# A decoder's first stage: operands loaded channels first, a halved first unit, and squares taken later

## The reference

```python
# first block, twice
h = rms_norm(x, norm_g[l])
proj = h @ w_in[l]                 # q_a, k_a, v_a, z_a, c_q, c_kv, k_r, z_b
...                                # differential and latent attention
x = x + mixed @ w_out[l]
# final norm of the first block, then the second block
m = rms_norm(mem, g_mem)           # mem: 256 tokens of width 2048, an input
kv = m @ w_kv                      # 2048 x 1024
...                                # convolution, pooling, cross attention on kv
x = x + mix @ w_out_2
h = rms_norm(x, g_ffn)
...                                # gated feed-forward with a short convolution
out = rms_norm(x, g_final)
```

## Time and profile before

| what | value |
|---|---|
| median of three runs | 1939.41 us |
| the profiled execution | 1939.58 us |
| its span | 1937.7 us |
| TensorE busy | 1923.2 us (99%) |
| VectorE busy | 1443.3 us (74%) |
| ACT busy | 1074.4 us (55%) |
| bytes moved by DMA | 357.09 MB, mean 184 GB/s |

### The profile page before, as it was taken

The page is one execution under the profiler, slowest core; times in us unless marked ns, Lnnn a source line. Parts: engine busy times, 40 slices in busy tenths (PEclk is TensorE's granted clock), DMA queues, the critical chain, the costliest instruction groups (busy, mean ns, idle before and its releaser), DMA issues.

```text
span 1937.7 us, 26740 instructions
## 1 busy us (share of the span) xinstructions
PE 1923.2 (99%) x9785; PEld 1630.7 (84%) x9785; DVE 1443.3 (74%) x2065; ACT 1074.4 (55%) x1575; POOL 46.3 (2%) x73
## 2 busy tenths in 40 slices
PE   8999999999999999999999999999999999999998
PEld 7888888888888888888888888888888888888886
DVE  7877676656777675656768766888877887889897
ACT  5545676654444676654544544555555555555554
POOL 1000030000000020000100000000000000000000
PEclk9999999999999999999999999999999999999999
DMA  8755455555655555545666455566666656676664
GB/s 310 236 199 171 143 155 157 145 162 184 199 205 177 148 153 177 159 152 178 216 192 187 155 166 187 181 193 185 192 187 188 190 185 187 192 224 190 205 211 148
DMA packets 246965, 357.09 MB, mean 184 GB/s; under 512 B 15318, under 2 KB 136496, under 8 KB 246364
## 3 DMA queue, kind: packets, MB, share of 16 engines
q1 hardware_dynamic: 245148, 349.08, 57.8%
q0 software_dynamic: 1584, 6.54, 1.0%
q10 hardware_dynamic: 144, 0.26, 0.0%
HBM read 352.69 MB, written 3.16 MB: 184 GB/s over the span
## 4 chain that ended last, share of the span: by engine, by line
PE 95%; DVE 4%; DMA 0%; ACT 0%; issue 0%; SPq 0%; ACTq 0%; DVEq 0%
PE acc L454 22%; PE acc L447 11%; PE acc L431 11%; PE acc L433 11%; PE acc L432 11%; PE acc L1181 4%; PE acc L1180 4%; PE acc L1182 4%; PE aux L511 2%; PE acc L1439 2%; PE acc L1441 2%; PE acc L1440 2%; DVE sb_w_lo L744 1%; DVE sb_down_lo L744 1%; PE aux L1111 1%; PE aux L1092 1%
## 5 line engine op out<-in xcount | busy, mean ns | idle before, releaser
L394 DVE TENSOR_TENSOR sb_w_lo<-sb_stage,sb_w_hi 128x1024 fp32r<-128x1024 f32 x477 | 584.0, 1227 | 272.3 <-ACT sb_w_hi L389 265.4
L389 ACT ACTIVATE sb_w_hi<-sb_stage 128x1024 fp32r<-128x1024 f32 x477 | 503.2, 1057 | 360.9 <-PE acc L447 123.1
L454 PE MATMUL acc<-sb_xT,sb_w_hi 128*128 128x512 f32 x1856 | 445.7, 391 | 0.0
L454 PEld LDWEIGHTS acc<-sb_xT,sb_w_hi 128*128 128x128 f32 x1856 | 340.8, 188 | 65.8
L447 PEld LDWEIGHTS acc<-sb_xT,sb_w_lo 128*128 128x128 f32 x1856 | 238.7, 191 | 9.3
L447 PE MATMUL acc<-sb_xT,sb_w_lo 128*128 128x256 f32 x1856 | 243.0, 283 | 0.0
L431 PE MATMUL acc<-sb_w_hi,sb_mT 128*128 128x512 f32 x560 | 224.9, 402 | 0.0
L433 PE MATMUL acc<-sb_w_hi,sb_mT 128*128 128x512 f32 x560 | 218.6, 390 | 0.0
L432 PE MATMUL acc<-sb_w_lo,sb_mT 128*128 128x512 f32 x560 | 218.4, 390 | 0.0
L431 PE MATMUL acc<-sb_w_hi,sb_xT 128*128 128x512 f32 x384 | 155.9, 406 | 0.0
L433 PE MATMUL acc<-sb_w_hi,sb_xT 128*128 128x512 f32 x384 | 150.1, 391 | 0.0
(11 more groups left out here) (418 smaller groups left out, 2839.3 us busy)
## 6 DMA issues: line engine op xcount, KB each, us to landing
sb_stage<-w_in SPq DMA_DIRECT2D x232, 512.0 KB, 4.1
sb_stage<-w_up SPq DMA_DIRECT2D x176, 512.0 KB, 3.8
sb_stage<-w_out SPq DMA_DIRECT2D x96, 512.0 KB, 3.9
sb_stage<-w_down SPq DMA_DIRECT2D x54, 512.0 KB, 6.8
sb_pair_stage<-w_down SPq DMA_DIRECT2D x34, 512.0 KB, 5.8
sb_stage<-w_kv SPq DMA_DIRECT2D x16, 512.0 KB, 6.8
sb_kvb<-w_in SPq DMA_DIRECT2D x16, 512.0 KB, 5.9
sb_stage<-w_ukv SPq DMA_DIRECT2D x16, 512.0 KB, 3.9
```

Source lines behind the costliest of these rows:

```text
L389: act.activation(w_hi[:, j % RING, 0:size], stage[:, j % RING, 0:size], ACT.Copy).then_inc(hi_ready, 1)
L394: dve.tensor_tensor(w_lo[:, j % RING, 0:size], stage[:, j % RING, 0:size], w_hi[:, j % RING, 0:size].bitcast(F32), ALU.subtract).then_inc( ...
L454: mm = pe.matmul(acc[:, 2 * pair + c, :], hi[:, k, c * P:(c + 1) * P], both, start=first and k == 0, stop=last and k == 3)
```

## The change

Three inputs now come from the host in another layout: `par` (all norm weights, channels first, 128 x 138), `par_ffn` (the same for the feed-forward's convolution) and `mem_T` and `x_T` (mem and x as 128 channels x 16 tiles x 256 tokens). The identity moves to POOL's queue. mem and x are rounded straight from these, two channel tiles at a time, with the gain as the scale; no turn of mem or of x before layer 0 remains. The first unit is loaded, rounded and multiplied in two halves, units 1 and 2 in an order that takes the rest of the weights last; TensorE multiplies zeros 18 times before. `par` and the first mem part are issued by ACT. x by tokens is loaded behind rows 4 to 7 of layer 0, and its squares are taken there. kv is copied unscaled by ACT. mem by tokens is loaded in layer 0's out projection, behind a wait for `gated`; its squares and 1/rms follow there, and `mkv` is scaled in unit 9 of the second block.

```diff
@@ TensorE @@
-                pe.transpose(acc[:, 2, 0:G_ROWS], par_rows, ident[0:G_ROWS, 0:G_ROWS]).then_inc(par_filled, 1)
...
-                for g in range(2):
-                    turn_in(g)
-                    for i in range(WARM[g]):
-                        pe.transpose(acc[:, 3, 0:P], ident[:, :], ident[:, :])
+                pe.wait_ge(warm_ready, 1)
+                for i in range(WARM):                
+                    pe.matmul(acc[:, 3, 0:P], warm, warm, start=True, stop=True)
+                def first_product():
...
+                    for k in range(2):
...
+                        pe.wait_ge(hi_ready if k else first_hi, 1)
+                        pe.wait_ge(mem_hi, k + 1)
+                        for t in range(T):
+                            pe.matmul(acc[:, t, :], m_hi(t), hi[:, k, :], start=k == 0, stop=False)
+                        pe.wait_ge(lo_ready if k else first_lo, 1)
+                        for t in range(T):
+                            pe.matmul(acc[:, t, :], m_hi(t), lo[:, k, :], start=False, stop=False)
+                        pe.wait_ge(mem_lo, k + 1)
+                        for t in range(T):
+                            mm = pe.matmul(acc[:, t, :], m_lo(t), hi[:, k, :], start=False, stop=False)
+                    mm.then_inc(unit_used, 1)
...
+                first_product()
+                for j in range(1, BY_PARTS):
+                    product_by_parts(j)
+                for j in range(BY_PARTS, U_MEM):
                     c, i = j // 8, j % 8
                     if c == 0:
-                        pe.wait_ge(turn_lo, i + 1)
+                        pe.wait_ge(mem_lo, 2 * i + 2)
...
-                    if j == 0:
-                        turn_in(2)
-                    if j < 5 or 6 <= j < 12:
-                        turn_in(3 + j if j < 5 else 2 + j)
...
@@ SP @@
+                sp.dma_start(stage[:, 0, 0:512], w_kv2[:, 0, 0:512]).then_inc(first_loaded, 16)
+                sp.dma_start(stage[:, 0, 512:UNIT], w_kv2[:, 1, 0:512]).then_inc(staged[0], 16)
+                for j in range(1, U_MEM):
                     c, k = j // 8, 2 * (j % 8)
                     if j < 8:
-                        cols = slice(j * 256, (j + 1) * 256)
-                        sp.dma_start(mem[:, :, cols], by_token(dram["mem_2"])[:, :, cols]).then_inc(mem_loaded[j], 16)
+                        sp.dma_start(raw_T[:, 2 * j:2 * j + 2, :], dram["mem_T"][:, 2 * j:2 * j + 2, :])\
+                          .then_inc(mem_loaded[j], 16)
                     load(sp, 0, j, w_kv2[:, k:k + 2, c * 512:(c + 1) * 512], 512)
...
+                    if j >= 8:
+                        g = j - 8
+                        sp.wait_ge(mem_lo, 2 * g + 2)
+                        sp.dma_start(raw_T[:, 2 * g:2 * g + 2, :], dram["x_T"][:, 2 * g:2 * g + 2, :])\
+                          .then_inc(x_turned[g], 16)
...
+                            if layer == 0 and c == 1 and i % 2 == 1:
+                                sp.wait_ge(gated, 8)
+                                cols = slice(i // 2 * 512, (i // 2 + 1) * 512)
+                                sp.dma_start(mem[:, :, cols], by_token(dram["mem_2"])[:, :, cols])\
+                                  .then_inc(mem_rows[i // 2], 16)
@@ ACT @@
+                act.dma_start(par[:, :], dram["par"]).then_inc(par_loaded, 16)
+                act.dma_start(raw_T[:, 0:2, :], dram["mem_T"][:, 0:2, :]).then_inc(mem_loaded[0], 16)
+                def round_raw(g, dst, first_gain, loaded, done):
+                    act.wait_ge(loaded[g], 16)
+                    for k in range(2 * g, 2 * g + 2):
+                        act.activation(dst[:, k, 0, :], raw_T[:, k, :], ACT.Copy,
+                                       scale=par[:, first_gain + k:first_gain + k + 1]).then_inc(done, 1)
...
@@ VectorE @@
+                def rest_raw(g, dst, first_gain, rounded, done):
+                    for k in range(2 * g, 2 * g + 2):
+                        dve.wait_ge(rounded, k + 1)
+                        dve.scalar_tensor_tensor(out=dst[:, k, 1, :], in0=raw_T[:, k, :],
+                                                 scalar=par[:, first_gain + k:first_gain + k + 1],
+                                                 in1=dst[:, k, 0, :].bitcast(F32), op0=ALU.mult, op1=ALU.subtract)\
+                           .then_inc(done, 1)
...
-                        if j == 4:
+                        if j == (4 if layer else 13):
                             x_rstd(step, dve, layer * SQ_PRO + SQ_PRO)
...
+                        for c, at in enumerate((QKV_END[0] if layer else 14, QKV_END[1])):
```

More of the change, by code:

```diff
@@ new lines, in product_by_parts @@
+                def product_by_parts(j):
+                    hi, lo = (w[:, j % RING, :].rearrange("p (k n) -> p k n", n=512) for w in (w_hi, w_lo))
+                    both = [(k, t) for k in range(2) for t in range(T)]
+                    m_part = lambda k, h, t: mT[:, 2 * j + k, h, t * P:(t + 1) * P]
+                    pe.wait_ge(hi_ready, j + 1)
+                    pe.wait_ge(mem_hi, 2 * j + 2)
+                    for k, t in both:
+                        pe.matmul(acc[:, t, :], m_part(k, 0, t), hi[:, k, :], start=False, stop=False)
+                    pe.wait_ge(mem_lo, 2 * j + 2)
+                    for k, t in both:
+                        pe.matmul(acc[:, t, :], m_part(k, 1, t), hi[:, k, :], start=False, stop=False)
+                    pe.wait_ge(lo_ready, j + 1)
+                    for k, t in both:
+                        mm = pe.matmul(acc[:, t, :], m_part(k, 0, t), lo[:, k, :], start=False, stop=False)
+                    mm.then_inc(unit_used, 1)
@@ L1230, in _ @@
                             qkv_seven(u)
-                        if u in (2, 3):
-                            pe.wait_ge(x_loaded[3], 16)
+                        if layer > 0 and u in (2, 3):
                             evacuated(pe, pairs, -1)
@@ L1532, in _ @@
                         act.activation(dots[:, :], dots[:, :], ACT.Exp).then_inc(exp_dots, 1)
-                    if 10 <= j < 16:
-                        square_x(x_step, act, (j - 10) // 2, ((j - 10) % 2,))
+                    if j == 10:
+                        multiplied(act, 0, 7)
+                        for t in range(T):
+                            ins = act.activation(mem_kv1[:, t, 0:512], acc[:, t, :], ACT.Copy)
+                        ins.then_inc(acc_free[0], 1)
+                x_first = Steps(act, x_squared)
                 for layer in range(LAYERS):
@@ L1636, in _ @@
                                 rounded(j - LEAD)
-                        if u == 1:
+                        if layer == 0 and u == 1:
+                            multiplied(act, 0, U_MEM - 1)
+                            for t in range(T):
+                                ins = act.activation(mem_kv1[:, t, 512:1024], acc[:, 2 + t, :], ACT.Copy)
+                            ins.then_inc(acc_free[1], 1)
+                        if layer == 0 and 5 <= u < 13:
+                            c, t = divmod(u - 5, 2)
+                            act.wait_ge(x_loaded[c], 16)
+                            square_x(x_first, act, c, (t,))
+                        if layer > 0 and u == 1:
                             evacuated(act, pairs, -1)
                             square_x(Steps(act, x_squared, layer * SQ_PRO + 6), act, 3)
-                        if u in (2, 3):
+                        if layer > 0 and u in (2, 3):
                             turn_round(act, tb0 + (u - 2), token_part(xT, 3, u - 2, 0))
@@ L1695, in _ @@
                             square_x(x_step, act, c - 1)
+                        if layer == 0 and c > 0 and 4 <= i < 7 and 3 * (c - 1) + i - 4 < 8:
+                            part, t = divmod(3 * (c - 1) + i - 4, 2)
+                            act.wait_ge(mem_rows[part], 16)
+                            m_step(act.activation(junk[:, :], mem[:, t, part * 512:(part + 1) * 512], ACT.Square,
+                                                  accum_out=sumsq_m[:, t, part:part + 1]))
                 def copy_half(half, base, j, pair, pairs_now, c):
@@ L1741, in _ @@
                         turn_round(act, TB2 + u, token_part(xT, 3, u, 0))
+                    if u == 9:
+                        act.wait_ge(mix_loaded, 16 * (2 + N_PIECES))
+                        for t in range(T):
+                            ins = act.activation(mkv[:, t, :], mkv[:, t, :], ACT.Copy, scale=rstd_m[:, t:t + 1])
+                        ins.then_inc(mkv_scaled, 1)
                     if u in (10, 11):
@@ L2118, in _ @@
                                       token_part(xT, c - 1, i - 2, 1))
+                        if layer == 0 and u == 30:
+                            dve.wait_ge(m_squared, 8)
+                            step(dve.tensor_reduce(sumsq_m2[:, :], sumsq_m[:, :, :], AX_X, ALU.add))
+                            rsqrt(step, dve, rstd_m[:, :], sumsq_m2[:, :], T, D)
                         if i == 7:
```

195 lines of the change are left out of this document (79 added, 116 removed).

## The result

The changed kernel takes **1946.25 us** (median of 9, 1945.21 to 1946.47) against 1939.69 of the kernel before beside it; ratio **1.0033**, 95% interval [1.0023, 1.0042]. It is slower by 6.6 us where 10.4 us of gain were forecast. The profiled execution took 1946.34 us.

A forecast was written before the change was run, and what follows sets the result against it. TensorE's product stream was taken to bound the kernel (95% of the chain). Turns and transposes gone, 7.4, plus an earlier start, 3.1, made 10.5, cross-checked at 10.7; 1939.58 - 10.6 = 1929.0 us, range 1927.0 to 1932.0.

The forecast's parts named there:

- The sum: Whole kernel: gains of 7.4 and 3.1 us, cross-checked at 10.7, taken as 10.6 off 1939.58, giving 1929.0 us.
- full to the tail: After the head: TensorE has no idle time to the end, so all of the 10.6 us gain should reach it.
- What moves: Squares, copies, scaling and loads moved to other stages and engines: hidden where they go, costed at 0.
- for a loss of over 6.7 us somewhere unseen: Place not named: a loss leaving no change (0.03) or a slower kernel; chance 0.04 in all.
- The slower rival: First layer's out projection: SP's wait for gated delays next weights, deciding from 4.9 us more delay; over 0.2% slower; chance 0.02.
- Turns gone: Up to the first layer's units 2 and 3: 14 turns at 0.48 us and five parameter transposes, 0.66, saved; 7.4 together.
- The head: Kernel start: after 18 matmuls on zeros the product stream begins at 7.8 us instead of 10.87, gaining 3.1.
- head shorter: Kernel start: clock rises by 4.6 us, so the warm-up ends near 6.8; 1928.0 us in all; chance 0.07.
- Early starvation: First units' loads: costed at 0 (0 to 1.5); as rival, unit 4 late by 1.5 us, 1930.9 in all; chance 0.13.
- The first layer's bank: First layer, unit 16: bank free at 105.95, needed at 106.35, 0.4 us spare, cost 0 to 1; bank-wait rival's chance 0.08.

The follow-up runs named there:

- e9_pad192: The changed kernel with 192 unused bytes behind neg_lam, so that late_T, mT and act_T begin 256 bytes behind their old places: 1929.55 us.
- e1_home: The changed kernel with small tiles sumsq_m2 and rstd_m put as views into neg_lam's tile, so the large tiles start at their old addresses: 1929.22 us.
- e2_before_64: The kernel before the change with only an unused tile of 64 bytes per partition added behind neg_lam, ahead of mT: 1955.43 us.
- e10_weights64: e1_home with 64 unused bytes ahead of w_hi and 192 behind w_lo, so only these weight halves stand off a multiple of 256: 1935.39 us.
- e8_warm30: e1_home with 30 warm-up matmuls on zeros at the start in place of 18: 1931.90 us.

## Why the prediction was wrong

**The step that failed** is the end of "The sum": "Afterwards TensorE is full to the tail, so all of it should reach the end", and behind it the list in "What moves", which costs moved instructions and DMAs and has no term for two tiles that the diff moves by name. TensorE was full, and slower. The unlisted term measured 17.0 us (1946.25 - 1929.22; 16.7 by e9_pad192, 15.7 as the pad in the kernel before), 1.6 times the gain, and takes the forecast from 1929 to 1946. No rival had it; the 0.04 left "for a loss of over 6.7 us somewhere unseen" is where it fell. "Full to the tail" had a smaller fault of its own: behind the 4% of VectorE in the earlier trace rows is the bank wait of the down products (0.85 us at 1818.04), which is there in e1_home too.

The slower rival named in its place, SP's wait for `gated`, did come as a wait of 5.6 us in SP's queue, and cost nothing. VectorE's timeline, SP's waits (us in total, times, longest) and SP's timeline of the kernel after, in the first layer's out projection:

```profile
417.58 1.29 DVE L2044 TENSOR_TENSOR sb_kvb<-sb_kvb,sb_kz 128x512 f32<-128x512 f32 x2 [1.51 <-ACT sb_kvb L1630]
```

```profile
SPq L908 <- DVE sb_kvb L2044: 5.6, 1, 5.6
```

```profile
418.90 0.37 SPq L908 DMA_DIRECT2D sb_kz<-mem  x1
419.31 0.47 SPq L387 DMA_DIRECT2D sb_stage<-w_out  x1
```

The weights went out 0.4 us behind the wait's end, and TensorE has no wait there.

The rest of the sum can be read in e1_home, which is the change with that term taken away. Its 1929.22 us is nearly the forecast 1929.0, in part by luck:

- **Turns gone, 7.4.** TensorE's timeline of the kernel before has its first product here:

```profile
10.52 0.77 PE L431 MATMUL acc<-sb_w_hi,sb_mT 128*128 128x512 f32 x1
```

  From there to the first layer's start it is 61.83 - 10.52 = 51.31 us before, 52.20 - 6.96 = 45.24 in e1_home and 52.58 - 7.99 = 44.59 in e9_pad192. So 6.1 and 6.7 us came of the 6.4 forecast there (12 turns at 0.48 and 0.66), the smaller one with the wait of 0.34 in it. The two turns behind that mark: 10.54 at the second block less 9.63, 0.9 against 2 x 0.48. Right.
- **The head, 3.1.** The sum took a start on the timeline (7.8) from the chain's 10.87. Read alike, it is 10.52 less 7.93, 2.6 us, in the kernel after. In the nine profiled runs with 18 zeros ahead the first product stands at 6.76 to 7.99 (e1_home 6.96: the rival "head shorter"), 7.37 in the mean, mostly by the moment at which the warm-up's pace doubles (3.95 to 7.15 us; 6.6 was taken). The mean gain is then 3.15: two errors, 0.35 in the base and 0.4 in the start, cancel. That is luck, the more so as the base moves too: it is 10.11 in e2_before_64.
- **Early starvation, 0 (0 to 1.5).** 0.34 us of waiting at unit 5 in e1_home, none in the kernel after and in e9_pad192, which start a microsecond later. In ACT's timeline of the kernel after unit 4 is rounded at 15.58, after a wait of 1.30 for its load; 16.4 was forecast.
- **The first layer's bank, 0.4 us to spare.** VectorE's timeline of the kernel after:

```profile
94.23 1.23 DVE L817 TENSOR_TENSOR sb_w_lo<-sb_stage,sb_w_hi 128x1024 fp32r<-128x1024 f32 x1
95.38 1.40 DVE L499 TENSOR_SCALAR sb_qa<-acc,sb_rstd 128x512 f32<-128x512 f32 x2
```

The bank is free at 96.78, and unit 16, which needs it, starts at 97.59, with no wait: 0.8 us to spare where 0.4 was forecast (0.7 in e1_home, 94.99 and 95.72). The step was right and its margin about as thin as said.

## What to carry to other kernels

A diff that adds, removes or moves an allocation, however small, moves every tile behind it; before costing anything else, list the base addresses of the tiles that the bounding engine reads, before and after, and see whether one has left a multiple of 256 bytes (shown here for float32r matmuls). Give the big operand tiles their places first, or pad to a multiple, and put small tiles behind them or inside each other. If a kernel is slower with no wait to show for it, divide a run of identical instructions' starts by their number and compare that with the other kernel: a modelled or mean length won't show it.

## What was unexpected of the hardware

- A float32r matmul of 128 x 512 whose 128 x 128 operand tile starts 64 or 128 bytes off a multiple of 256 follows the last by 231 to 236 ns instead of 227, 2 to 4%. A 512-wide operand off it costs 2 to 3 ns at 64 bytes (229.9 to 230.3 for mT; 229 in the mean of w_hi and w_lo, where the intervals from w_lo's starts don't grow) and 5 at 128 (232.9 for mT). seven_x, 32 or 96 bytes off, is at 231 to 234. 192 and 224 bytes off were not tried.
- For 256 columns the sign turns: 113 ns off the multiple (128 x 128 operand in w_lo), 120 on it. All 1,856 of them together gave back 10.4 us in e10_weights64, where 8.4 were lost on the matmuls of 512 columns with the same kind of operand in w_hi. So aligning isn't best for every shape, and a version with w_lo alone off the multiple might gain; it was not run.
- The slower pace outlasts its cause: by three matmuls behind a 128 x 128 operand off the multiple, by up to ten behind a wide one. Ten intervals of the same lengths (224 to 236) also follow the wait that ends at 1807.75 in e1_home, where both operands are on a multiple, so a short stretch of them is no sign of the place.
- After a wait of 2.01 us (2.4 from start to start), in the middle of a stream that had been full, eight matmuls ran at the 1.2 GHz level in e8_warm30 (0.43 us apart); behind the same wait, 1.10 us long in e1_home, the granted clock stays at 1.00.
- 64 unused bytes cost a tuned kernel 15.7 of 1939.7 us, more than the whole change was worth.
